# Expert gates of the second 128 tokens: scattered through DRAM in place of one-hot products

## Chip, cores and metric

One core of a Trainium2 chip runs the whole kernel. The metric is the device time of one execution in microseconds, the median of several runs.

## What is computed

A streaming encoder of two layers on 256 tokens of 1024 values. Each layer has an attention mixer and then a channel mixer, product-key expert retrieval (PEER), which the change is about. Cut to that:

```python
q = einsum('td,de->te', xt, w_q).reshape(t, 8, 2, 128)
sc = einsum('thpd,hpnd->thpn', q, sub_keys)            # 8 heads, 2 sides, 128 keys
v1, i1 = top_k(sc[:, :, 0], 16);  v2, i2 = top_k(sc[:, :, 1], 16)
cand = v1[..., :, None] + v2[..., None, :]
top_v, top_pos = top_k(cand.reshape(t, 8, 256), 16)
eidx = (i1 * 128 + i2) at top_pos                      # 16384 experts
gates = softmax(top_v, axis=-1)
a = gelu(einsum('tkd,td->tk', u_tab[eidx], xt)) * gates
out = einsum('tk,tkd->td', a, v_tab[eidx])
```

Each token has 8 heads x 16 = 128 experts of 16384. An expert is a pair of keys (i1, i2).

## The kernel before, in words

The kernel gathers nothing. It computes all 16384 experts for all tokens and multiplies by a gate matrix that is zero where an expert was not chosen. The experts are walked in 128 tiles, a tile j holding the 128 experts of one second key. Tiles go through two stages in each layer.

**Up stage.** For tile j, SyncE loads the tile of u (512 KB) into one of four buffers `raw`; ScalarE rounds it to the upper part `hi` (`split`, line 1119), VectorE takes the remainder `lo` (`lower`, line 1550), and TensorE multiplies both with the tokens (`x_both`, upper and lower part). Tiles 0 to 55 are "wide": one product of 512 columns and one of 256 for each of 8 slices, 16 in all, and VectorE adds the two halves (`sum_halves`, line 1618). Tiles from 56 are "up" tiles with 24 products of 256 columns. After Gelu on ScalarE, SyncE stores the tile's 128x256 result in DRAM (`spill`, to `s_store`). A tile's u is loaded when the subtraction for the tile four before is done, its split is two tiles ahead of TensorE.

**Down stage.** For each tile SyncE fetches the stored activations and a tile of v, VectorE multiplies by the gates (`weigh`, line 1562), and TensorE accumulates 12 products of 512 columns. In layer 0 the weights of layer 1 are loaded into the freed parts of the gate matrix at the same time, by GpSimd's queue.

**The gate matrix** `gates` takes all of the big buffer `big` (128 partitions x 128 tiles x 256 tokens, 16.8 MB): the first key runs over partitions, the second over tiles j. It can be written only when the retrieval's scratch, which lies in the same buffer, is no longer needed. It is made so:

- *Retrieval* on VectorE (`retrieve_head`, `top16`): the best 16 of each side and of the candidates, for 8 heads. It is cut into pieces that are issued between the subtractions of the tiles, by a generator (`retrieval`, `advance(500)` twice a step; a piece yields its nominal nanoseconds, and a step takes pieces until 500 are reached).
- *Selection* (`choose`, line 1506): the place of each chosen pair among the top 16 of either side is turned into keys by 32 selections `q_hots` of 128x256 values each (line 1533), and the gates by an Exp on ScalarE (line 1202, ahead of wide tile 52) and a division.
- *Sums* (`picks`, line 793): behind up tile 57, TensorE adds the 16 selections of each side in 64 bf16 products of 128 columns and so turns them, and the gates by two transposes, to have the 128 chosen experts on partitions and the tokens along the row. VectorE copies the three results into `pick`.
- *Groups* (`one_hot` line 1552, `group` line 837, `copy_gates` line 1156): for four tokens VectorE writes one-hot matrices of the first key and, times the gates, of the second; TensorE multiplies the two with one product of 128x128x128 for each token; ScalarE copies the four 128x128 results into `gates`. There are 64 groups, one in each up tile from tile 60 (`GROUP_AT`) to 123.

**Order around the change.** SyncE's queue issues loads of u, spills, loads of v and fetches in program order, with a wait ahead of each. GpSimd's queue issues the loads of the projection weights, `w_out`, the keys and `w_q`, and is idle while a layer's tiles run, but for layer 1's weights in layer 0's down stage. ScalarE and VectorE run a fixed order by tile; VectorE's first `weigh` follows the last subtraction of the up stage and a wait for all groups' copies (`g_copied`). Products are recorded under the helper's line 541.

Of the kernel before, what the change touches and what calls it, by code (L numbers as in the profile page):

```python
# [41 lines left out]
GROUPS = T // 4  # L42
GROUP_AT = 60
EXP_AT = 52
# [22 lines left out]
C_END = 3 * P  # L67
# [112 lines left out]
def build(nc, a, out):  # L180

    with ExitStack() as ctx:
# [23 lines left out]
        pick = wmod_ring[:, 2, 0:3 * T].rearrange("p (a t) -> p a t", a=3)  # L206
# [14 lines left out]
        iota = cst[:, C_IOTA:C_IOTA + P]  # L221

# [43 lines left out]
        s_store = nc.dram_tensor("s_store", (NKEY, P, T), F32, kind="Internal").ap()  # L266
        gates = big[:].rearrange("p (j t) -> p j t", j=NKEY)
# [26 lines left out]
        def q_area(at, size, **kw):  # L294
# [14 lines left out]
        q_idf = q_area(Q_IDF, 512, t=TT, h=PH, s=2, k=TOPK)  # L309
        q_ab = [q_area(at, 256).bitcast(U32) for at in (Q_A, Q_B, Q_TMP, Q_TMP + 256)]  # L310
        q_tmp = [q_area(Q_TMP + 256 * n, 256) for n in (2, 3, 4)]
        q_abf = [q_area(Q_AF, 256, t=TT, n=P), q_area(Q_BF, 256, t=TT, n=P)]
# [33 lines left out]
                 "q_ps", "q_copied", "key_ps", "key_copied", "sel_ready", "pick_copied",  # L346
                 "hot_ready", "hot_used", "g_copied", "hi_done", "lo_done", "w_used",
                 "s_gelu", "a_ready", "ah_done", "al_done",
                 "e_act", "e_dve", "eT_ps", "x_done")
        s = [{n: sem(f"{n}_{l}") for n in names} for l in range(LAYERS)]  # L350
        for n in ("s_half", "s_sum", "oh_done", "ol_done", "o_used", "yh_done", "yl_done", "xh_done", "xl_done", "gate_max", "gate_exp", "pick_ready", "pick_ps"):
            s[0][n] = s[1][n] = sem(n)
# [4 lines left out]
        mod_kept = sem("mod_kept")  # L357
        norm_names = ("sq_ready", "ss_ps", "rec_ready", "root_ready", "rms_ready", "rms_ps", "hat_ready", "h_ready")
# [18 lines left out]
        def _(sp):  # L377
# [16 lines left out]
            for l in range(LAYERS):  # L394
# [93 lines left out]
        def _(pool):  # L488
            for l in range(LAYERS):
# [34 lines left out]
                for h in range(PH):  # L524
# [10 lines left out]
                    pool.dma_start(big[:, at:at + 2 * D], a["w_q"][l, :, h * 2 * D:(h + 1) * 2 * D]).then_inc(wq_in[h % WQ_RING], 16)  # L535


        @block.tensor
        def _(pe):
# [212 lines left out]
            def queries(l):  # L752
                def sub_scores(h):
                    pe.wait_ge(s[l]["q_copied"], 2 * h + 2)
                    pe.wait_ge(keys_in, 16 * (l + 1))
                    if h >= 2:
                        pe.wait_ge(s[l]["key_copied"], h - 1)
# [34 lines left out]

            def picks(l):
                pe.wait_ge(ident_ready, 1)
                for n in range(4):
                    t, side = n // 2, n % 2
                    pe.wait_ge(s[l]["sel_ready"], TOPK * (side + 1))
                    c = side * T + t * P
                    for k in range(TOPK):
                        mm(bank[6][:, c:c + P], q_hot[n][:, k].rearrange("p h k -> p (h k)"), ident_bf, k == 0, k == TOPK - 1)  # L800
                pe.wait_ge(s[l]["pick_ready"], l + 1)
                for t in range(TT):
                    last = nc.tensor.transpose(bank[7][:, t * P:(t + 1) * P], q_g[:, t].rearrange("p h k -> p (h k)"), ident)
                last.then_inc(s[l]["pick_ps"], 1)

            def experts(l):
# [84 lines left out]
            def expert_out(l):  # L891
                for m in range(KT):
                    if m % 4 == 0:
                        pe.wait_ge(s[l]["e_act"], 1 + m // 4)
                        pe.wait_ge(s[l]["e_dve"], 1 + m // 4)
# [41 lines left out]
        def _(act):  # L937
# [30 lines left out]
            def norm(i, out_halves=()):  # L968
                if i == 0:
                    act.wait_ge(x_in, 16)  # L970
                for k in range(KT):
                    for q in out_halves[2 * max(k - 2, 0):2 * max(k - 1, 0)] if k >= 4 else out_halves[k:k + 1]:
                        split_out(i // 2, q)
                    if i:
                        act.wait_ge(s[(i - 1) // 2]["x_mixed" if i % 2 else "x_done"], k + 1)
# [99 lines left out]
            for l in range(LAYERS):  # L1075
# [91 lines left out]
                def copy_keys(h):  # L1167
                    act.wait_ge(s[l]["key_ps"], h + 1)
                    f(q_key[:, h].rearrange("p s t n -> p (s t n)"), bank[6 + h % 2][:, :], ACT.Copy).then_inc(s[l]["key_copied"], 1)

                for h in range(PH):
                    for side in range(2):
# [12 lines left out]
                        if h >= 2:  # L1185
                            act.wait_ge(s[l]["key_ps"], h - 1)
# [11 lines left out]
                with act.Fori(1, EXP_AT // 4) as i:  # L1198
                    for r in range(4):
                        wide_step(4 * i + r, r, i)  # L1200
                act.wait_ge(s[l]["gate_max"], l + 1)
                f(q_e[:], q_e[:], ACT.Exp).then_inc(s[l]["gate_exp"], 1)
                for n in range(EXP_AT, WIDE_TILES):
                    wide_step(n, n % 4, n // 4)
                sum_gelu(WIDE_TILES - 1, (WIDE_TILES - 1) % 4)
                up_steps(WIDE_TILES, GROUP_AT)
                act.wait_ge(s[l]["pick_copied"], 2)
                with act.Fori(0, GROUPS // 4) as i:
                    for r in range(4):
                        up_step(GROUP_AT + 4 * i + r, r, i + GROUP_AT // 4)  # L1210
                        copy_gates(4 * i + r, r)
                for r in range(4):
# [22 lines left out]
        def _(dve):  # L1235
# [256 lines left out]
            def retrieve_head(l, h):  # L1492
                dve.wait_ge(s[l]["key_copied"], h + 1)
# [12 lines left out]
            def choose(l):  # L1506

                v.tensor_tensor(q_e[:], q_top[:], q_top[:, :, :, 0:1].to_broadcast([P, TT, PH, TOPK]), ALU.subtract)\
                    .then_inc(s[l]["gate_max"], 1)

                pos = q_pos[:].rearrange("p t h k -> p (t h k)")
                far, d1, d2 = q_tmp
                v.tensor_single_scalar(q_ab[0], pos, 4, ALU.logical_shift_right)
                yield 600
                v.tensor_single_scalar(q_ab[1], pos, 15, ALU.bitwise_and)
                v.tensor_single_scalar(q_ab[2], pos, 2, ALU.logical_shift_right)
# [338 lines left out]
```

## Time and profile before

| what | before |
|---|---|
| time, median of 3 runs | 2010.26 us (2008.14 to 2011.47) |
| span of the profiled execution | 2004.7 us (5.6 under the median: what lies around the span) |
| TensorE busy | 1966.7 us, 98% |
| VectorE busy | 1554.3 us, 78% |
| ScalarE busy | 1104.4 us, 55% |
| GpSimd busy | 28.2 us, 1% |
| DMA moved | 446.88 MB, mean 223 GB/s |

The profile shows one execution. Busy time of an engine counts its instructions alone; matmuls are pipelined, so an engine that is always busy may still differ in how many products it ends in a time, and the period from one tile to the next says more. The DMA share is the mean busy share of the core's 16 DMA engines.

### The profile page before, as it was taken

To read this page: it belongs to the slowest core of one execution; us is meant where nothing else is said; L and a number is where in the kernel's file an instruction comes from. 1 tells how busy PE (TensorE), PEld (TensorE's weight loads), DVE (VectorE), ACT (ScalarE), POOL (GpSimd) and SP (SyncE) were. 2 spreads that over 40 slices of the span, in tenths; PEclk is the share of its full clock that TensorE was granted. 3 is DMA by queue.
4 is the path that set the end of the run, shared out by engine and by line. 5 is a ranking of instruction groups with operands and counts; after the bars stand their busy time and mean duration, and the time that the engine had idled before them with its cause. 6 is when DMAs were issued, how large, how long until landed. Compare 5 with 4: busy or idle time off the path is not lost.

```text
span 2004.7 us, 42800 instructions
## 1 busy us (share of the span) xinstructions
PE 1966.7 (98%) x12066; PEld 1740.0 (87%) x12066; DVE 1554.3 (78%) x3993; ACT 1104.4 (55%) x2231; POOL 28.2 (1%) x57
## 2 busy tenths in 40 slices
PE   7989999999999999999999999999999999999998
PEld 6748988899999888888888798889999998888887
DVE  5666799987777688888876568998777767777776
ACT  2035466655555555555555555666555555555554
POOL 1000000000000000000000000000000000000000
PEclk9999999999999999999999999999999999999999
DMA  9961299765556799999830435776555567777774
GB/s 368 375 234 50 93 311 299 264 189 174 177 170 174 255 337 339 331 342 331 292 119 1 190 127 178 236 237 207 178 174 172 175 207 240 241 240 243 239 243 164
DMA packets 171104, 446.88 MB, mean 223 GB/s; under 512 B 19088, under 2 KB 85904, under 8 KB 166944
## 3 DMA queue, kind: packets, MB, share of 16 engines
q1 hardware_dynamic: 163520, 392.65, 60.4%
q0 software_dynamic: 7520, 53.45, 6.9%
q8 instruction: 32, 0.52, 0.1%
q14 instruction: 32, 0.26, 0.0%
HBM read 409.32 MB, written 36.70 MB: 222 GB/s over the span
## 4 chain that ended last, share of the span: by engine, by line
PE 93%; DMA 2%; DVE 2%; ACT 2%; issue 1%; SPq 0%; DVEq 0%; ACTq 0%
PE bank L541 93%; DMA big<-in_w_mod 1%; ACT big L1050 1%; DMA big<-in_w_out 1%; DVE lo L1550 0%; DVE big L1533 0%; DMA raw<-in_v 0%; PE bank L677 0%; DVE raw L1264 0%; ACT hi L1119 0%; DVE big L1366 0%; DVE big L1272 0%; ACT hi L999 0%; DVE work L1618 0%; ACT raw L988 0%
## 5 line engine op out<-in xcount | busy, mean ns | idle before, releaser
L1550 DVE TENSOR_TENSOR lo<-raw,hi 128x512 fp32r<-128x512 f32 x1024 | 706.6, 690 | 274.5 <-ACT hi L1119 262.4
L541 PE MATMUL bank<-x_both,hi 128*128 128x256 f32 (+1 forms) x3984 | 886.8, 311 | 2.9 <-ACT x_both L966 1.5
L1119 ACT ACTIVATE hi<-raw 128x512 fp32r<-128x512 f32 x1024 | 643.9, 629 | 415.9 <-PE bank L541 388.3
L541 PE MATMUL bank<-x_both,lo 128*128 128x256 f32 x2440 | 685.8, 281 | 0.0
L541 PEld LDWEIGHTS bank<-x_both,hi 128*128 128x128 f32 x3984 | 647.4, 191 | 43.7 <-issue 2.4
L541 PEld LDWEIGHTS bank<-x_both,lo 128*128 128x128 f32 x2440 | 463.6, 190 | 0.0
L541 PE MATMUL bank<-hi,a_hi 128*128 128x512 f32 x1024 | 398.7, 389 | 1.5 <-DVE lo L1550 1.5
L541 PE MATMUL bank<-lo,a_hi 128*128 128x512 f32 x1024 | 398.6, 389 | 0.0
L541 PE MATMUL bank<-hi,a_lo 128*128 128x512 f32 x1024 | 398.5, 389 | 0.0
L541 PEld LDWEIGHTS bank<-hi,a_hi 128*128 128x128 f32 x1024 | 192.2, 188 | 41.6 <-issue 1.6
L541 PEld LDWEIGHTS bank<-hi,a_lo 128*128 128x128 f32 x1024 | 192.2, 188 | 39.9
L541 PEld LDWEIGHTS bank<-lo,a_hi 128*128 128x128 f32 x1024 | 192.2, 188 | 39.9
L1558 DVE TENSOR_SCALAR wmod_ring<-cst,wmod_ring 128x128 f32<-128x128 f32 x512 | 142.4, 343 | 0.0
L541 PE MATMUL bank<-wmod_ring 128*128 128x128 f32 x1024 | 135.2, 275 | 0.0
L541 PEld LDWEIGHTS bank<-wmod_ring 128*128 128x128 f32 x1024 | 125.7, 192 | 0.0
L1143 ACT ACTIVATE work<-bank 128x256 f32<-128x256 f32 x144 | 55.1, 382 | 112.7 <-PE bank L541 112.7
L1564 DVE TENSOR_TENSOR wmod_ring<-wmod_ring,big 128x256 f32<-128x256 f32 x256 | 107.5, 421 | 1.1
L541 PE MATMUL bank<-raw,big 128*128 128x256 f32 (+1 forms) x464 | 104.4, 383 | 3.7 <-ACT raw L988 3.7
L1569 DVE TENSOR_TENSOR a_lo<-wmod_ring,a_hi 128x256 fp32r<-128x256 f32 x256 | 107.2, 419 | 0.0
L541 PEld LDWEIGHTS bank<-raw,big 128*128 128x128 f32 (+1 forms) x464 | 85.7, 188 | 21.0 <-issue 8.3
L1165 ACT ACTIVATE a_hi<-wmod_ring 128x256 fp32r<-128x256 f32 x256 | 103.0, 403 | 0.0
L1555 DVE TENSOR_TENSOR wmod_ring<-cst,wmod_ring 128x512 f32<-128x512 f32 x128 | 87.6, 685 | 0.0
(161 smaller groups left out, 1330.0 us busy)
## 6 DMA issues: line engine op xcount, KB each, us to landing
raw<-in_u SPq DMA_DIRECT2D x256, 512.0 KB, 4.0
raw<-in_v SPq DMA_DIRECT2D x256, 512.0 KB, 4.6
s_store<-work SPq DMA_DIRECT2D x256, 128.0 KB, 3.7
wmod_ring<-s_store SPq DMA_DIRECT2D x256, 128.0 KB, 3.7
wmod_ring<-in_w_mod SPq DMA_DIRECT2D x54, 512.0 KB, 5.7
big<-in_w_mod SPq DMA_DIRECT2D x40, 512.0 KB, 6.4
big<-in_w_q POOLq DMA_DIRECT2D x16, 1024.0 KB, 7.4
big<-in_w_in POOLq DMA_DIRECT2D x5, 2048.0 KB, 21.4
```

Source lines behind the costliest of these rows:

```text
L541: return nc.tensor.matmul(o, w, x, start=start, stop=stop, skip_group_check=free)
L1050: last = f(c, c, ACT.Exp, bias=neg[:, 2 * i + t:2 * i + t + 1], accum_out=den[:, 2 * i + t:2 * i + t + 1])
L1119: f(hi[:, r % 2, c], raw[:, r, c], ACT.Copy).then_inc(s[l]["hi_done"], 1)
L1143: f(work[:, r, :], bank[4 + r % 2][:, 0:T], ACT.Gelu).then_inc(s[l]["s_gelu"], 1)
L1165: f(a_hi[:, r % 2, :], back[:, b, :], ACT.Copy).then_inc(s[l]["ah_done"], 1)
L1550: v.tensor_tensor(lo[:, r % 2, c], raw[:, r, c], hi[:, r % 2, c].bitcast(F32), ALU.subtract).then_inc(s[l]["lo_done"], 1)
L1555: v.tensor_tensor(hot[r % 2][:, 0], iota.unsqueeze(1).to_broadcast([P, 4, P]), pick[:, 0, bass.ds(4 * g, 4)].unsqueeze(2).to_broadcast([P, ...
L1558: ins = v.tensor_scalar(hot[r % 2][:, 1, n, :], iota, pick[:, 1, bass.ds(4 * g + n, 1)], pick[:, 2, bass.ds(4 * g + n, 1)], ALU.is_equal, ...
L1564: v.tensor_tensor(back[:, b, :], back[:, b, :], gates[:, bass.ds(j, 1), :].rearrange("p a t -> p (a t)"), ALU.mult)\
L1569: v.tensor_tensor(a_lo[:, r % 2, :], back[:, b, :], a_hi[:, r % 2, :].bitcast(F32), ALU.subtract).then_inc(s[l]["al_done"], 1)
```

## The change

The tokens 128 to 255 ("far") no longer pass through one-hot products. Their gates are added into a DRAM matrix `g_store` (8.4 MB, one for each layer), which SyncE has cleared before, by indirect DMAs on GpSimd's queue: one for each of the 128 chosen experts, which adds one gate of each of the 128 tokens at the place computed for it. Each head's 16 wait for the 16 of the head before. Then 16 loads bring the matrix into the far half of `gates`. The first 128 tokens keep the one-hot groups, now 32, from tile 68 to 99.

The selection goes in two waves of four heads, each right behind its heads' retrieval; the first wave's sums for far tokens are taken by TensorE ahead of wide tile 24, and VectorE computes places (`far_places`) at a fixed piece of head 4's retrieval. Each wave has its own Exp, ahead of tiles 16 and 60. VectorE waits for all far loads ahead of the first `weigh`. The far sums keep the tokens on partitions: the identity is the stationary operand and 64 columns of selections move.

Semaphores that had one counter for each layer now share one for both, so that their waits count on; the ring of descriptors of GpSimd's DMAs is set to 8192 bytes. In both layers the clear is one DMA of a 128x512 tile of zeros, repeated.

```diff
-GROUPS = T // 4
-GROUP_AT = 60
-EXP_AT = 52
+GROUPS = P // 4
+GROUP_AT = 68
+SCATTERED = T - P
+EXP_AT = (16, 60)
+FAR_PLACES_AT = (4, 9)
+SUM_AT = 24
+GATE_LOADS = 16
+ZERO_COLS = 512
...
+                def clear(n):
+                    sp.dma_start(g_store[n].rearrange("(a p f) o -> p a (f o)", p=P, f=ZERO_COLS),
+                                 zero[:].unsqueeze(1).to_broadcast([P, NKEY * SCATTERED // ZERO_COLS, ZERO_COLS])).then_inc(zeroed, 16)
+
                 if l == 0:
                     sp.wait_ge(s[0]["mod_tile"], NMOD)
                     sp.wait_ge(s[0]["map_max"], 16)
+                    sp.wait_ge(zero_ready, 1)
+                    sp.wait_ge(s[0]["prob_ready"], 2)
+                    clear(0)
                 sp.wait_ge(s[l]["x_mixed"], KT)
...
                 sp.dma_start(raw[:, 0:2].rearrange("p a n -> p (a n)"), x_store).then_inc(x_back, 16)
+                if l == 0:
+                    clear(1)
...
+            def scatter(l):
+
+                for h in range(PH):
+                    if h % 4 == 0:
+                        pool.wait_ge(s[l]["far_ready"], 4 * l + 2 * (h // 4 + 1))
+                    if h == 0:
+                        pool.wait_ge(zeroed, 16 * (l + 1))
+                    else:
+                        pool.wait_ge(s[l]["far_done"], 16 * TOPK * (PH * l + h))
+                    for k in range(TOPK):
+                        c = h * TOPK + k
+                        pool.indirect_dma_start(g_store[l], bass.IndirectOffsetOnAxis(ap=far_at[:, c:c + 1], axis=0), far_gate[:, c:c + 1], None,
+                                                compute_op=ALU.add).then_inc(s[l]["far_done"], 16)
+                pool.wait_ge(s[l]["far_done"], 16 * TOPK * PH * (l + 1))
+                pool.wait_ge(s[l]["pick_copied"], l + 1)
+                for n in range(GATE_LOADS):
+                    j = slice(n * NKEY // GATE_LOADS, (n + 1) * NKEY // GATE_LOADS)
+                    pool.dma_start(gates[:, j, P:T], g_store[l].rearrange("(j p t) o -> p j (t o)", j=NKEY, p=P)[:, j]).then_inc(s[l]["far_in"], 16)
...
+                scatter(l)
...
+            def far_sums(l, w):
+
+                pe.wait_ge(ident_ready, 1)
+                pe.wait_ge(s[l]["sel_ready"], 2 * TOPK * (2 * l + w + 1))
+                for side in range(2):
+                    o = bank[6][:, (2 * w + side) * 64:(2 * w + side + 1) * 64]
+                    for k in range(TOPK):
+                        last = mm(o, ident_bf, q_hot[2 + side][:, k, 4 * w:4 * w + 4].rearrange("p h k -> p (h k)"), k == 0, k == TOPK - 1)
+                last.then_inc(s[l]["far_ps"], 1)
...
+                far_sums(l, 1)
+                for side in range(2):
                     for k in range(TOPK):
-                        mm(bank[6][:, c:c + P], q_hot[n][:, k].rearrange("p h k -> p (h k)"), ident_bf, k == 0, k == TOPK - 1)
...
+                        mm(bank[7][:, side * P:(side + 1) * P], q_hot[side][:, k].rearrange("p h k -> p (h k)"), ident_bf, k == 0, k == TOPK - 1)
+                pe.wait_ge(s[l]["pick_ready"], 2 * l + 2)
+                nc.tensor.transpose(bank[7][:, 2 * P:3 * P], q_g[:, 0].rearrange("p h k -> p (h k)"), ident).then_inc(s[l]["pick_ps"], 1)
...
-                with pe.Fori(1, WIDE_TILES // 4) as i:
+                with pe.Fori(1, SUM_AT // 4) as i:
+                    for r in range(4):
+                        wide(4 * i + r, r)
+                far_sums(l, 0)
+                with pe.Fori(SUM_AT // 4, WIDE_TILES // 4) as i:
...
+                def gate_exps(w):
+                    act.wait_ge(s[l]["gate_max"], 2 * l + w + 1)
+                    c = q_e[:, :, 4 * w:4 * w + 4]
+                    f(c, c, ACT.Exp).then_inc(s[l]["gate_exp"], 1)
...
+                        v.scalar_tensor_tensor(out=q_hots[:, :, side, k, hs], in0=q_abf[side][:, w].rearrange("p t (h k) -> p t h k", k=TOPK), scalar=float(k),
+                                               in1=q_idf[:, w, :, :, side, k:k + 1].to_broadcast([P, TT, 4, TOPK]),
                                                op0=ALU.is_equal, op1=ALU.mult).then_inc(s[l]["sel_ready"], 1)
                         if k % 2:
-                            yield 800
...
+                            yield 500
...
+            def far_places(l, w):
+
+                dve.wait_ge(s[l]["far_ps"], 2 * l + w + 1)
+                o = bank[6][:, 2 * w * 64:2 * (w + 1) * 64].rearrange("p (s n) -> p s n", s=2)
+                link(v.tensor_scalar(far_tmp[:], o[:, 1], float(P * SCATTERED), row, ALU.mult, ALU.add))
+                v.scalar_tensor_tensor(out=far_at[:, 64 * w:64 * w + 64], in0=o[:, 0], scalar=float(SCATTERED), in1=far_tmp[:],
+                                       op0=ALU.mult, op1=ALU.add).then_inc(s[l]["far_ready"], 1)
...
+                        for n, took in enumerate(retrieve_head(l, h)):
+                            yield took
+                            if (h, n) == FAR_PLACES_AT:
+                                far_places(l, 0)
+                                yield 400
+                        if h % 4 == 3:
+                            yield from choose(l, h // 4)
...
                 dve.wait_ge(s[l]["g_copied"], GROUPS)
+                dve.wait_ge(s[l]["far_in"], 16 * GATE_LOADS * (l + 1))
```

## Rows read from the trace of the kernel before

**Rows 1.** The page: busy time of each engine; chain that ended last.

```profile
PE 1966.7 (98%) x12066; PEld 1740.0 (87%) x12066; DVE 1554.3 (78%) x3993; ACT 1104.4 (55%) x2231; POOL 28.2 (1%) x57
...
PE 93%; DMA 2%; DVE 2%; ACT 2%; issue 1%; SPq 0%; DVEq 0%; ACTq 0%
```

**Rows 2.** Windows by stage: engines' busy us (x instructions), PEclk, DMA share, GB/s.

```profile
150.00:191.00 41.00, 38.46 (x302) 35.92 (x302) 23.87 (x49) 20.25 (x40) 0.00 (x0) 1.00 0.06 24
...
250.00:400.00 150.00, 150.00 (x866) 130.78 (x865) 146.41 (x461) 100.51 (x213) 0.00 (x0) 1.00 0.87 290
...
425.00:665.00 240.00, 240.00 (x2041) 240.00 (x2040) 187.07 (x449) 135.76 (x255) 0.00 (x0) 1.00 0.59 175
...
700.00:1000.00 300.00, 300.00 (x1326) 248.41 (x1325) 256.88 (x579) 173.51 (x332) 11.61 (x22) 1.00 0.94 329
...
1030.00:1075.00 45.00, 43.72 (x305) 41.50 (x303) 25.10 (x49) 23.28 (x46) 0.00 (x0) 0.92 0.01 1
...
1230.00:1370.00 140.00, 140.00 (x810) 122.41 (x809) 133.20 (x449) 95.18 (x205) 0.00 (x0) 1.00 0.74 236
```

**Rows 3.** TensorE's timeline: first wide tile, two groups, two tiles without groups.

```profile
251.80 0.48 PE L541 MATMUL bank<-x_both,hi 128*128 128x512 f32 x1
...
428.98 1.06 PE L541 MATMUL bank<-wmod_ring 128*128 128x128 f32 x8
...
432.74 1.06 PE L541 MATMUL bank<-wmod_ring 128*128 128x128 f32 x8
...
670.04 0.40 PE L541 MATMUL bank<-x_both,hi 128*128 128x256 f32 x2
...
672.92 0.40 PE L541 MATMUL bank<-x_both,hi 128*128 128x256 f32 x2
```

**Rows 4.** Groups of instructions by form: busy us, mean ns.

```profile
L541 PE MATMUL bank<-wmod_ring 128*128 128x128 f32 x1024 | 135.2, 275 | 0.0
...
L1550 DVE TENSOR_TENSOR lo<-raw,hi 128x512 fp32r<-128x512 f32 x1024 | 706.6, 690 | 274.5 <-ACT hi L1119 262.4
...
L1533 DVE SCALAR_TENSOR_TENSOR big<-big 128x256 bf16<-128x256 f32 x64 | 24.4, 427 | 0.0
...
L1498 DVE TENSOR_TENSOR big<-big 128x128 f32<-128x128 f32 x16 | 4.6, 286 | 0.1
...
L1202 ACT ACT_TABLE_LOAD x2 | 2.6, 1283 | 0.0
...
L535 POOL DMA_DIRECT2D big<-in_w_q x16 | 8.4, 528 | 156.1 <-PE bank L541 156.1
```

**Rows 5.** TensorE's timeline: sums of the selections, layers 0 and 1.

```profile
417.43 2.85 PE L541 MATMUL bank<-par,big 128*128 128x128 bf16 x48 [1.82 <-DVE big L1533]
...
1379.63 3.75 PE L541 MATMUL bank<-par,big 128*128 128x128 bf16 x64
```

**Rows 6.** VectorE's timeline: second normalisation of layer 0.

```profile
140.22 2.15 DVE L1407 TENSOR_SCALAR big<-big,stat 128x128 f32<-128x128 f32 x8
```

**Rows 7.** Instructions on x_store: ns min/median/max, first and last start.

```profile
L415 SPq DMA_DIRECT2D x_store<-raw x2: 327/327/327, 191.0 to 1157.5; - x2
```

**Rows 8.** DMA issues: count, KB each, median us to landing.

```profile
raw<-in_u SPq DMA_DIRECT2D x256, 512.0 KB, 4.0
...
out_yT<-raw SPq DMA_DIRECT2D x4, 256.0 KB, 2.2
...
stat<-in_c SPq DMA_DIRECT2D x1, 4.0 KB, 1.6
```

**Rows 9.** DMA packets of 1275 to 1300 us, then of 275 to 300 us.

```profile
DMA packets 2579, 5.84 MB, mean 234 GB/s; under 512 B 289, under 2 KB 1441, under 8 KB 2579
...
q1 hardware_dynamic: 2579, 5.84, 73.3%
...
DMA packets 2997, 7.38 MB, mean 295 GB/s; under 512 B 333, under 2 KB 1482, under 8 KB 2997
...
q1 hardware_dynamic: 2997, 7.38, 90.6%
```

More of the change, by code:

```diff
@@ L66 @@
 C_ID, C_ONE, C_IOTA = 0, P, 2 * P
-C_END = 3 * P
+C_ROW = 3 * P
+C_END = C_ROW + 1
 def win_cols(l):
@@ L221, in build @@
         iota = cst[:, C_IOTA:C_IOTA + P]
+        row = cst[:, C_ROW:C_ROW + 1]
         def selector(h):
@@ L266, in build @@
         s_store = nc.dram_tensor("s_store", (NKEY, P, T), F32, kind="Internal").ap()
+        g_store = [nc.dram_tensor(f"g_store{l}", (NKEY * P * SCATTERED, 1), F32, kind="Internal").ap() for l in range(LAYERS)]
         gates = big[:].rearrange("p (j t) -> p j t", j=NKEY)
@@ L974, in norm @@
                     if i:
-                        act.wait_ge(s[(i - 1) // 2]["x_mixed" if i % 2 else "x_done"], k + 1)
+                        act.wait_ge(s[(i - 1) // 2]["x_mixed" if i % 2 else "x_done"], k + 1 if i % 2 else KT * ((i - 1) // 2) + k + 1)
                     if i or k >= 4:
@@ L1197, in _ @@
                     wide_step(n, n, 0, False, n >= 1)
-                with act.Fori(1, EXP_AT // 4) as i:
+                def gate_exps(w):
+                    act.wait_ge(s[l]["gate_max"], 2 * l + w + 1)
+                    c = q_e[:, :, 4 * w:4 * w + 4]
+                    f(c, c, ACT.Exp).then_inc(s[l]["gate_exp"], 1)
+                with act.Fori(1, EXP_AT[0] // 4) as i:
                     for r in range(4):
                         wide_step(4 * i + r, r, i)
[L1201 to L1204, printed above, removed]
+                gate_exps(0)
+                with act.Fori(EXP_AT[0] // 4, WIDE_TILES // 4) as i:
+                    for r in range(4):
+                        wide_step(4 * i + r, r, i)
                 sum_gelu(WIDE_TILES - 1, (WIDE_TILES - 1) % 4)
-                up_steps(WIDE_TILES, GROUP_AT)
-                act.wait_ge(s[l]["pick_copied"], 2)
+                up_steps(WIDE_TILES, EXP_AT[1])
+                gate_exps(1)
+                up_steps(EXP_AT[1], GROUP_AT)
+                act.wait_ge(s[l]["pick_copied"], l + 1)
                 with act.Fori(0, GROUPS // 4) as i:
@@ L1504, in retrieve_head, with choose, part @@
                                   for t in range(TT)])
[L1506 to L1523 removed]
+            def choose(l, w):
+                hs = slice(4 * w, 4 * w + 4)
+                c = slice(64 * w, 64 * w + 64)
+                def part(area):
+                    return area[:, 0:P].rearrange("p (t n) -> p t n", t=TT)
+                v.tensor_tensor(q_e[:, :, hs], q_top[:, :, hs], q_top[:, :, hs, 0:1].to_broadcast([P, TT, 4, TOPK]), ALU.subtract)\
+                    .then_inc(s[l]["gate_max"], 1)
+                pos = q_pos[:].rearrange("p t h k -> p t (h k)")[:, :, c]
+                far, d1, d2 = [part(x) for x in q_tmp]
+                ab = [part(x) for x in q_ab]
+                v.tensor_single_scalar(ab[0], pos, 4, ALU.logical_shift_right)
+                yield 400
+                v.tensor_single_scalar(ab[1], pos, 15, ALU.bitwise_and)
+                v.tensor_single_scalar(ab[2], pos, 2, ALU.logical_shift_right)
+                yield 400
+                v.tensor_single_scalar(ab[3], pos, 3, ALU.bitwise_and)
+                link(v.tensor_scalar(far, pos, float(WIDE * TOPK), None, ALU.is_ge))
+                yield 400
+                v.tensor_tensor(d1, ab[2], ab[0], ALU.subtract)
+                link(v.tensor_tensor(d2, ab[3], ab[1], ALU.subtract))
+                yield 500
@@ L1543, in choose @@
-                yield 1000
+                            yield 500
+                dve.wait_ge(s[l]["gate_exp"], 2 * l + w + 1)
+                total = gsum.rearrange("p (t h) -> p t h", t=TT)[:, :, hs]
+                share = grec.rearrange("p (t h) -> p t h", t=TT)[:, :, hs]
+                link(v.reduce_sum(total, q_e[:, :, hs], axis=AX_X))
+                link(v.reciprocal(share, total))
+                v.tensor_tensor(q_g[:, 0, hs], q_e[:, 0, hs], share[:, 0].unsqueeze(2).to_broadcast([P, 4, TOPK]), ALU.mult)\
+                    .then_inc(s[l]["pick_ready"], 1)
@@ new lines, in choose @@
+                v.tensor_tensor(far_gate[:, c].rearrange("p (h k) -> p h k", k=TOPK), q_e[:, 1, hs],
+                                share[:, 1].unsqueeze(2).to_broadcast([P, 4, TOPK]), ALU.mult).then_inc(s[l]["far_ready"], 1)
+                yield 700
+            def far_places(l, w):
[4 more added lines that the diff above has]
+                                       op0=ALU.mult, op1=ALU.add).then_inc(s[l]["far_ready"], 1)
```

76 lines of the change are left out of this document (31 added, 45 removed).

## The prediction

> **What bounds the kernel now.** Read first the page's busy line and chain: TensorE is busy 98% of 2004.7 us and holds 93% of the chain of waits that ended last [rows 1]. An instruction taken off TensorE is worth its full length, as long as nothing else becomes late. Next the windows by stage: in both expert stages TensorE is busy in all of every stretch, its granted clock 1.00, and the DMA engines' share runs from 0.59 to 0.94 [rows 2]. VectorE is nearly full in the first layer's wide tiles (146.4 of 150 us) but not in the group tiles (187 of 240). So the one-hot groups are paid for on TensorE, and the reserve that the change draws on is DMA time and GpSimd, which is all but idle (28 us).
>
> TensorE's timeline prices a group. Two groups of consecutive tiles start at 428.98 and 432.74, so a tile with a group takes 3.76 us; tiles without one start at 670.04 and 672.92, 2.88 us [rows 3]. A group costs 0.88 us.
>
> **The change part by part.** The sum is made against the profiled execution, whose span is 2004.7; the median of 2010.26 is 5.6 us (0.28%) over it, and I put the difference on top unchanged.
>
> *Groups.* 64 become 32 in each layer: 64 x 0.88 = 56.3 us less. The x1024 row holds all of them: 512 products, two records each [rows 4]. VectorE's one-hots and ScalarE's copies for them fall away too and were hidden.
>
> *Sums of the selections.* Before, 64 bf16 products take 3.75 us, 0.059 each [rows 5]. After, there are 32 of that form and 64 with half the columns, one transpose fewer. Half-width products cost between half and all of a full one: 0 to 1.9 us more a layer. I take 1.0, so +2. In layer 0 they were interrupted by 1.82 us of waiting for VectorE's selections [rows 5]; that wait may stay or go, I take 0.9 off.
>
> *Selection on VectorE.* From the code: 151 pieces of retrieval and selection become 175, spread two to a step over 66 steps instead of 58; as before, only the last one or two are left when the steps end. A 256-element selection takes 427 ns, a 128-element operation 286 [rows 4], so 64 x 286 replaces 32 x 427, 4.6 us more a layer, but each piece is cheaper and the eight added steps have room: two subtractions of 690 ns in a 2.88 us tile. If that cover failed, TensorE would wait up to those 4.6 us at the sums. I cost it at nothing.
>
> *New waits.* TensorE's first sums, before tile 24, need selections that VectorE issues in step 19 (layer 0) and 22 (layer 1); tile 24 itself needs step 22. VectorE's read of them stands at step 26 or 28, with the subtractions for later tiles queued behind, and two tiles of distance. ScalarE's first Exp at tile 16 needs step 7 or 13. Each Exp brings two table loads of 1.28 us [rows 4], so one more pair a layer on an engine with 50 of 150 us free [rows 2]: 0 to 2.6 us a layer, I take 0.3, +0.6.
>
> *Clearing.* 8.4 MB from SP in layer 0 goes out when the second normalisation ends, at 142.4; SP's next issue, the store of x, is at 191.0 [rows 6, 7]. The engines' share between 150 and 191 is 0.06 [rows 2]. At the 329 GB/s that the down stage moves [rows 2] it takes 26 us, w_q's and the keys' loads beside it (5.2 MB) 16 more: over by 185. The second clear goes behind the read of x at the layer's end, where the share is 0.01 to 1075. Nothing, in both; without that cover the store and the load of u behind it would be up to 26 us late.
>
> *Scatters.* On GpSimd, 64 a wave, behind w_q's issues and ahead of the next layer's weights, which wait for the down stage anyway. No row shows an indirect DMA. From below: a plain issue is 0.53 us [rows 4]. From above: issue plus landing of a small one, 0.53 + 1.6 for 4 KB, 0.53 + 2.2 for the output's [rows 4, 8]: 2.13 to 2.73. The sixteen of a head do not wait for each other, so the issue is the nearest row, but each has 128 addresses; I take 1.3, plus 2.2 at the end of each head: 64 x 1.3 + 9 = 92 us a wave. Wave one of layer 0 starts near tile 27, 251.8 + 27 x 2.77 (16 records a tile, 866 in 150 us) = 327, and ends at 419. Wave two starts after the second sums, 251.8 + 56 x 2.77 + 10 x 2.88 + 5 = 441, and ends at 534. The up stage, whose last tile ended at 672.92 + 2 x 2.88 = 679, will end near 651.
>
> *Loading back.* 16 loads, 8.4 MB in 16384 pieces of 512 B, between 534 and 651, beside u and the spills. Two windows price a packet: they differ by 377 of 4 KB and by 17.3% of 16 x 25 us, so 0.18 us each; the first then leaves 0.074 us for each of its 1152 packets of 1 KB [rows 9]. A 512 B packet costs between half and all of that: 38 to 76 us with all engines. Free are 0.41 of the 33 us with groups left and 0.29 of the 82 without (0.74 at 2.77 us a tile is 0.71 at 2.88): 37 us. By bytes there is more: 329 GB/s ran without hurting TensorE, which leaves 154 GB/s and 102 GB/s, 13.5 MB against 8.4. I take it to fit, near the lower price, at 2 us a layer for u's loads held up: +4.
>
> **Sum:** -56.3 + 2 - 0.9 + 0.6 + 4 = -50.6. Span 1954, time 2010.3 - 50.6 = **1960**. Without the loads' 4 it is 1956.
>
> **A rule weighed.** The rows say that a small transfer is nearly all overhead: 4 KB lands after 1.6 us, 512 KB after 4.0 [rows 8]. The Trainium skill ("DMA: Bandwidth & Descriptors", its rules for kernel authors) says the same, to coalesce because under 64 KB one pays mostly overhead, and its anatomy of the gpsimd path gives about 2.0 us fixed, most of it the landing's receipt. It speaks against 256 transfers of 512 bytes. Paid by each in turn it would make 128 x 2.0 = 256 us a layer, an estimate by that page, and give rival B; paid once a head, as I assume, it agrees with the sum.
>
> **Rivals.** A, the loads come late but the groups still win. At a packet price midway, 0.055, they need 56 us of engines against 37 free: VectorE's new wait ahead of the first gate product holds the down stage for 19 us a layer, 1956 + 38 = 1994. For it: spare engine time is no more than the lowest need. Against: the bytes.
>
> B, slower: GpSimd is the bound. If a scatter takes c, both waves of a layer run end to end from 327, 327 + 128c + 18. At 2.13 that is 618, the loads find 33 us with 10 us of engine time, 28 are left for after the last tile, and 1956 + 56 = 2012: no gain, which is the point from which it decides. At 2.4 the waves end at 652 and all 38 us lie open, 1956 + 2 x 39 = 2034, the time I give B; at 2.73 they end at 694, 2 x 81 more, 2118. For it: 2.13 is only issue plus one landing, and VectorE holds two 690 ns subtractions in each tile; a scatter that had to let one pass would cost 1.3 + 0.69 = 1.99, just short of the point. The Trainium skill ("SBUF — State Buffer", who interferes with whom) has such a rule: a VectorE instruction with two SBUF inputs blocks a GpSimd instruction that reads SBUF; no run here shows it. Against B: the code queues sixteen at a time.
>
> C, the change does not do what it says: the saved TensorE time goes to another engine. A tile without a group asks 2 x 0.69 us of VectorE against 2.88 of TensorE, ScalarE is busy 136 of 240 us even with groups [rows 2], and such tiles do run at 2.88, so only a coincidence of small losses gives 2010.
>
> **How the numbers follow.** Sum right, 0.47, with its own range 1949 (no cost for sums, Exp and loads, the wait gone, a little less pressure on VectorE) to 1972. A 0.20, B 0.27, C 0.06. The range reaches to A and to B as priced, up to 2035, which leaves out B's dearer prices, under 0.2. Within 0.2% (4 us, about what a measurement of this kernel can tell from none) is C: 0.06; faster 0.67; slower 0.27.
>
> **What would show it.** In the after trace: 512 records of the group product in place of 1024; up tiles without groups at 2.88; POOL's indirect issues with a mean under 1.6 us; the last gate load landing before the last up tile ends, with no gap of TensorE behind it. A gap there, put down to a DMA into big, is A or B: A if the second wave's last scatter was issued by about 540, B if near 620 or later. Wrong altogether: group tiles that stay at 3.76 where only u runs, u's loads landing much later than 4.0 us in the stretch of the loads, or a wait of TensorE before tile 24.

## The result, and the profile after

The changed kernel takes **2012.6 us** in the median of 8 runs, the kernel before 2007.7 in 8 runs beside it: ratio 1.0031, 95% interval 1.0019 to 1.0042, a little slower. The forecast was 1960, faster. What came is rival B, GpSimd as the bound, at the time of the point from which it decides (2012) and not at the time it was given (2034). The profiled executions have spans of 2009.3 and 2004.7 us.

The page of the changed kernel, busy time and chain of waits [rows 1]:

```profile
PE 1916.6 (95%) x11616; PEld 1687.5 (84%) x11616; DVE 1462.3 (73%) x3779; ACT 1121.2 (56%) x2217; POOL 482.7 (24%) x346
...
PE 58%; POOL 21%; issue 10%; DMA 6%; DVE 3%; ACT 2%; SPq 0%; ACTq 0%; DVEq 0%; POOLq 0%
```

TensorE has 50.1 us less to do (1966.7 - 1916.6). But the chain, 93% TensorE before, now runs through GpSimd for a fifth of the span. The windows of the up and down stage of layer 0 show where the gain is paid back (columns as in [rows 2]):

```profile
425.00:665.00 240.00, 227.41 (x1936) 226.48 (x1934) 147.17 (x326) 125.43 (x236) 156.23 (x102) 0.98 0.84 214
...
625.00:650.00 25.00, 24.12 (x199) 23.77 (x199) 11.73 (x17) 12.25 (x25) 9.45 (x11) 1.00 1.03 356
650.00:675.00 25.00, 6.91 (x58) 6.70 (x56) 1.39 (x2) 2.77 (x6) 1.84 (x3) 0.69 0.99 327
675.00:700.00 25.00, 22.32 (x87) 18.26 (x88) 18.76 (x41) 12.49 (x25) 1.10 (x2) 0.84 0.68 222
```

TensorE stands nearly still from 656 to 678 us while the DMA engines are busy in all of the stretch. Its timeline there, and the row of layer 1:

```profile
656.63 0.28 PE L585 MATMUL bank<-x_both,lo 128*128 128x256 f32 x1
677.68 0.76 PE L585 MATMUL bank<-hi,a_hi 128*128 128x512 f32 x1 [20.78 <-ACT a_hi L1218]
678.25 0.63 PE L585 MATMUL bank<-lo,a_hi 128*128 128x512 f32 x1
678.67 0.63 PE L585 MATMUL bank<-hi,a_lo 128*128 128x512 f32 x1
...
1645.09 0.77 PE L585 MATMUL bank<-hi,a_hi 128*128 128x512 f32 x1 [27.78 <-ACT a_hi L1218]
```

The first products of the down stage come 20.8 and 27.8 us after TensorE was ready, and the first dozen (nine in layer 1) 0.43 us apart instead of 0.23: the granted clock is 0.69 in the window with the gap and 0.84 in the next, a mix of its two levels of 1.2 and 2.4 GHz, after TensorE had been idle. VectorE's waits name the cause, GpSimd's timeline shows it being made:

```profile
DVE wmod_ring L1644 <- DMA big<-g_store: 49.7, 2, 27.4
```

```profile
331.98 1.65 POOL L523 DMA_INDIRECT g_store<-far_gate,far_at  x1 [109.33 <-DVE far_at L1622]
...
484.08 1.54 POOL L523 DMA_INDIRECT g_store<-far_gate,far_at  x1 [2.43 <-DMA g_store<-far_gate,far_at]
...
615.90 1.54 POOL L523 DMA_INDIRECT g_store<-far_gate,far_at  x1 [0.30 <-issue]
617.75 1.76 POOL L523 DMA_INDIRECT g_store<-far_gate,far_at  x1 [0.31 <-issue]
622.12 6.29 POOL L529 DMA_DIRECT2D big<-g_store  x7 [2.61 <-DMA g_store<-far_gate,far_at]
643.95 6.13 POOL L529 DMA_DIRECT2D big<-g_store  x7 [15.55 <-issue]
667.93 1.76 POOL L529 DMA_DIRECT2D big<-g_store  x2 [17.84 <-issue]
```

The 128 scatters of layer 0 run without a pause between the waves (the second begins at 484) from 332 to 618, the 16 loads behind them are issued from 622 to 670 in three batches, and the last lands near 675, 18 us after the last up tile ended. The group of all scatters, by form, gives their price:

```profile
L523 POOL DMA_INDIRECT g_store<-far_gate,far_at x256 | 425.5, 1662 | 372.0 <-DVE far_at L1622 223.5 <-issue 105.8 <-DMA g_store<-far_gate,far_at 42.6
```

That is 1.66 us each and 0.30 us of "issue" behind each (idle time for which the profile shows no cause). To this come 3.0 us of waiting at a head's end for the landing of its last scatter (42.6 in 14), and beyond the 0.30s some 34 us of stops inside heads (105.8 - 240 x 0.30, both layers).

### The profile page after: what moved, and what is told of

Its sections match the earlier page's. It is cut to its first block, busy times and chain, and to the rows that moved or that the text cites. A ratio compares the mean times of both kernels' runs of the same rounds, so it can differ in the third digit from the quotient of the medians.

```text
span 2009.3 us, 41296 instructions
## 1 busy us (share of the span) xinstructions
PE 1916.6 (95%) x11616; PEld 1687.5 (84%) x11616; DVE 1462.3 (73%) x3779; ACT 1121.2 (56%) x2217; POOL 482.7 (24%) x346
## 2 busy tenths in 40 slices
DMA packets 220811, 480.72 MB, mean 239 GB/s; under 512 B 56496, under 2 KB 123312, under 8 KB 216640
## 4 chain that ended last, share of the span: by engine, by line
PE 58%; POOL 21%; issue 10%; DMA 6%; DVE 3%; ACT 2%; SPq 0%; ACTq 0%; DVEq 0%; POOLq 0%
PE bank L585 57%; POOL g_store L523 20%; DMA g_store<-far_gate,far_at 3%; POOL big L529 1%; DVE lo L1630 1%; ACT big L1103 1%; DMA big<-in_w_out 1%; DMA big<-g_store 1%; DMA raw<-in_x 0%; DMA raw<-in_u 0%; PE bank L721 0%; DMA raw<-x_store 0%; ACT hi L1172 0%; DVE wmod_ring L1671 0%; DVE raw L1325 0%
## 5 line engine op out<-in xcount | busy, mean ns | idle before, releaser
L523 POOL DMA_INDIRECT g_store<-far_gate,far_at x256 | 425.5, 1662 | 372.0 <-DVE far_at L1622 223.5
L585 PE MATMUL bank<-hi,a_hi 128*128 128x512 f32 x1024 | 400.5, 391 | 48.6 <-ACT a_hi L1218 48.6
L1474 DVE TENSOR_TENSOR lo<-big,hi 128x512 fp32r<-128x512 f32 x76 | 52.1, 689 | 32.7 <-ACT hi L1010 32.4
L1638 DVE TENSOR_SCALAR wmod_ring<-cst,wmod_ring 128x128 f32<-128x128 f32 x256 | 73.2, 375 | 0.0
L585 PE MATMUL bank<-big 128*128 128x128 f32 (+5 forms) x368 | 59.4, 326 | 9.3 <-ACT big L1121 8.3
## 6 DMA issues: line engine op xcount, KB each, us to landing
g_store<-zero SPq DMA_DIRECT2D x2, 8192.0 KB, 30.7
```

What stands on the lines that cost most here:

```text
L523: pool.indirect_dma_start(g_store[l], bass.IndirectOffsetOnAxis(ap=far_at[:, c:c + 1], axis=0), far_gate[:, c:c + 1], None, compute_op=ALU ...
L585: return nc.tensor.matmul(o, w, x, start=start, stop=stop, skip_group_check=free)
L1474: v.tensor_tensor(lo[:, q % 4 // 2, c], narrow_half(l, q), hi[:, q % 4 // 2, c].bitcast(F32), ALU.subtract).then_inc(s[l]["ol_done"], 1)
L1638: ins = v.tensor_scalar(hot[r % 2][:, 1, n, :], iota, pick[:, 1, bass.ds(4 * g + n, 1)], pick[:, 2, bass.ds(4 * g + n, 1)], ALU.is_equal, ...
```

## Experiments

Times stand beside runs of the kernel before on the same chip, in three groups (medians 2005.6, 2005.4, 2005.2; the last experiment's single run beside 2005.7). Experiments 1, 4 and 6 have two runs, the others but the last four to eight. The changed kernel was not run beside them: the ratio to hold against theirs is its 1.0031.

**1. Half the scatters.** For each head only k = 0 to 7:

```
-                    for k in range(TOPK):
+                    for k in range(KEPT):        # KEPT = 8, the counts waited for accordingly
```

> Leaves out the scatters of the picks 8 to 15 of every head (half of the gates of the second 128 tokens); all else as after the change. Theory G (the chain on GpSimd: 128 scatters at 1.66 + 0.30 us, eight landings of about 3.6 us, then the loads, sets when the down stage starts): 64 scatters and eight landings are 154 us a layer, the second wave starts when its addresses are ready at about 450 and ends near 527, the loads end before 600, far ahead of the last up tile at 656; the gaps of TensorE ahead of the down stage (20.8 and 27.8 us) and the lower clock behind them go: 2011 - 49 - 5 = 1957. Rival E (the loads and the scatters cost TensorE its time because the DMA engines are full, wherever they stand): the loads hold up u's loads instead, the up stage gets 10 to 20 us longer a layer, 1977 to 1997.

Measured 1959.2 us, ratio 0.9767 (0.9725 to 0.9809). GpSimd's scatters of layer 0 (count, ns min/median/max, first and last start) and the windows where the gap was:

```profile
L524 POOL DMA_INDIRECT g_store<-far_gate,far_at x64: 1535/1544/2082, 335.5 to 521.8; - x64
```

```profile
625.00:650.00 25.00, 25.00 (x211) 25.00 (x210) 11.95 (x18) 13.44 (x27) 0.00 (x0) 1.00 0.80 239
650.00:675.00 25.00, 25.00 (x148) 22.25 (x147) 18.43 (x38) 14.63 (x29) 0.56 (x1) 1.00 0.95 317
```

As theory G has it: the loads are issued from 527 to 570, no gap is left, and the granted clock stays at 1.00. Loads that come this early cost TensorE nothing.

**2. Waiting for a quarter of the loads.**

```
-                dve.wait_ge(s[l]["far_in"], 16 * GATE_LOADS * (l + 1))
+                dve.wait_ge(s[l]["far_first"], 16 * FIRST_LOADS * (l + 1))     # 4 of 16
...
+                        if first:                                # ahead of down step 24 or 28
+                            dve.wait_ge(s[l]["far_in"], 16 * (GATE_LOADS - FIRST_LOADS) * (l + 1))
```

> Same outputs as the changed kernel: VectorE waits for 4 of the 16 loads ahead of the first gate product, for the other 12 ahead of the 26th (layer 0) or 30th (layer 1). Theory G: the first four loads are issued within 4 us of the last scatter's landing at 622 and land by about 640, before the last up tile at 656; the gap of both layers goes, the other twelve land by about 690, ahead of the tile that needs them (656 + 26 x 2.7 = 726): 1955 to 1962. Rival E (full DMA engines): the loads then compete with v's, s's and the modulation's, the first down tiles wait for DMA instead, and only part of the gap returns: 1975 to 2000.

1987.2 us, 0.9904 (0.9879 to 0.9928): half of what theory G expected, in rival E's range. TensorE's timeline in layer 0:

```profile
650.40 0.47 PE L586 MATMUL bank<-x_both,hi 128*128 128x256 f32 x2 [1.79 <-ACT work L1197]
...
655.29 0.48 PE L586 MATMUL bank<-x_both,hi 128*128 128x256 f32 x2 [1.79 <-ACT work L1197]
...
668.02 0.77 PE L586 MATMUL bank<-hi,a_hi 128*128 128x512 f32 x1 [5.26 <-DVE a_lo L1650]
```

Up tiles now follow each other in 4.89 us where 2.88 is normal, since u's tiles and the spills of s land late (ScalarE's waits there: 6.9 us on u, 7.2 on the spills, 9.7 on v), and 5.3 and 9.0 us of gap remain. So the start of the loads isn't all. That their rate is too much beside the rest is a suspicion here, which experiments 8 and 9 test.

**3. Twice the descriptor memory.**

```
-    nc = bacc.Bacc("TRN2", ..., dynamic_dma_scratch_size=8192)
+    nc = bacc.Bacc("TRN2", ..., dynamic_dma_scratch_size=16384)      # ZERO_COLS = 256 for room
```

> Twice the memory for GpSimd's DMA descriptors (16384 bytes a partition instead of 8192), and the clear written in pieces of 1 KB instead of 2 KB to make room; all else as after the change. Rival R (the ring of descriptors holds 7 of the loads and GpSimd idles 33 us a layer until it empties): 15 or 16 loads are issued in one go in about 14 us, the last lands about 33 us earlier, near 645, both gaps go, about 1960. Theory G with full engines under the loads (DMA share 1.0, 340 GB/s, of which u and the spills take about half): the issues come together, but the last load still lands within 5 us of 675, and the time stays within 2003 to 2013.

1993.6 us, 0.9946 (0.9928 to 0.9964): neither. GpSimd's timeline:

```profile
616.35 13.27 POOL L529 DMA_DIRECT2D big<-g_store  x15 [3.10 <-DMA g_store<-far_gate,far_at]
658.47 0.88 POOL L529 DMA_DIRECT2D big<-g_store  x1 [28.84 <-issue]
```

Fifteen loads instead of seven go out in one batch, so the memory does set the batch; the sixteenth waits 28.8 us. In 625 to 650 us the engines are full (1.03) and TensorE has 20.3 us of 25 where it had 24.1: part of what the gap gave back is taken from the up stage. Gaps of 4.1 and 6.3 us remain ahead of the down stages.

**4. Even and odd heads in two matrices**, so that a head waits for the head but one before it.

```
-                        pool.wait_ge(s[l]["far_done"], 16 * TOPK * (PH * l + h))
+                    if h >= 2:
+                        pool.wait_ge(s[l][f"far_done{h % 2}"], 16 * TOPK * (PH // 2 * l + h // 2))
```

> Even heads are added into one matrix of DRAM, odd heads into a second one that is cleared with it and not loaded back (leaves out half of the gates of the second 128 tokens); a head waits for the landing of the head but one before it. Rival B (the landings between heads are what is lost): the 6 of 8 landings between heads that held GpSimd, about 3.6 us each, go, scatters end about 22 to 25 us earlier, near 598, the loads end near 650, the gap of layer 0 goes and layer 1 keeps about 3: 1962 to 1968. If instead the scatters' own pace on GpSimd or the DMA engines' pace of 4-byte additions is the limit: the period rises above 1.96 us and the last scatter stays later than 612, 1990 to 2010. The second clear takes the engines 31 us longer near 150 and 1030 us and may hold up the store of x there by up to 12 us in layer 0; that is read from its own row and taken off.

1965.4 us, 0.9798 (0.9766 to 0.983).

```profile
L525 POOL DMA_INDIRECT g_store<-far_gate,far_at x64: 1534/1543/2562, 331.4 to 549.2; - x64
L525 POOL DMA_INDIRECT g_odd<-far_gate,far_at x64: 1542/1542/4143, 365.1 to 579.1; - x64
```

The last scatter starts at 579 instead of 618, 39 us earlier, more than the landings' 22: the stops inside heads are gone too. The store of x was issued at 190.7 and landed in 8.8 us at most, so the second clear cost at most 5 us there. One matrix, with its landings and stops together, thus costs a seventh of the scatters' 286 us.

The time lies in rival B's range, in part by luck: the scatters end 19 us sooner than it said, but the loads, issued from 585 on, take 4.3 us of TensorE's time out of the up stage of layer 0, with the engines full:

```profile
600.00:625.00 25.00, 21.81 (x178) 21.26 (x177) 9.69 (x14) 10.69 (x23) 6.13 (x7) 1.00 1.02 354
625.00:650.00 25.00, 23.90 (x197) 23.75 (x198) 12.47 (x18) 13.48 (x28) 1.76 (x2) 1.00 0.99 345
```

**5 to 7. Larger pieces.** The matrix laid out by partition and the gates on chip in blocks of eight rows, so that a load is 128 pieces of 4 KB instead of 1024 of 512 B:

```
-        gates = big[:].rearrange("p (j t) -> p j t", j=NKEY)
+        gates = big[:].rearrange("p (b s i t) -> p b s i t", b=GATE_LOADS, s=2, t=P)
...
-                    pool.dma_start(gates[:, j, P:T], g_store[l].rearrange("(j p t) o -> p j (t o)", j=NKEY, p=P)[:, j])
+                    pool.dma_start(gates[:, n, 1], g_store[l].rearrange("(p j t) o -> p j (t o)", p=P, j=NKEY)[:, j])
```

With the wait of the second experiment, then alone, then with that wait and the larger memory of the third:

> Same outputs as the changed kernel. The matrix in DRAM and the gates on chip are laid out so that a load is 128 pieces of 4 KB instead of 1024 of 512 B, and VectorE waits for 4 of 16 loads first, as in the second experiment (1987). Theory P (what the loads cost beside u is their 16384 pieces): the engines' need falls from some 29 to some 20 us (by 159 ns for a 4 KB packet), the ring no longer stops GpSimd, up tiles during the loads stay at 2.88 and the first gate product finds its loads landed: 1957 to 1968. Theory Y (it is bytes: up stage and loads together ask for more than the 350 GB/s that the engines moved there): the stretching of the last up tiles to 4.9 us per pair of half tiles and the late v loads stay, 1980 to 1990.

> Same outputs; only the layout of the experiment before (loads of 128 pieces of 4 KB), with one wait for all 16 loads as in the changed kernel. Theory P: 16 loads issued within 10 us of the last landing at 622, all landed by about 650, gaps of TensorE ahead of the down stage gone in layer 0 and under 8 us in layer 1: 1958 to 1975. Theory Y: 8.4 MB at the 130 GB/s that were left beside u need 64 us or take u's share; up tiles stretch and the gap stays in part: 1985 to 1997, as with the larger ring (1994).

> Same outputs; pieces of 4 KB, the wait for the first 4 loads, and the larger ring (with the clear in 1 KB pieces) together. The larger ring let the last scatter be issued 6 us earlier in layer 0 and 12 in layer 1 in the third experiment; if the start of the loads still decides, this one is 3 to 12 us faster than the one without it; if the loads are hidden already there, the same within 3 us.

1987.1 us, 0.9904 (0.9881 to 0.9927); 1990.5, 0.9921 (0.9901 to 0.9941); 1980.5, 0.9872 (0.9856 to 0.9889). The fifth and the sixth lie in theory Y's ranges. Beside the second experiment, pieces of 4 KB bring no time, though they move more while the engines are full. The same window of the second and of the fifth:

```profile
625.00:650.00 25.00, 22.60 (x187) 22.22 (x185) 9.70 (x14) 10.45 (x21) 9.69 (x11) 1.00 1.01 336
625.00:650.00 25.00, 24.21 (x202) 24.03 (x201) 10.52 (x16) 11.66 (x23) 7.30 (x15) 1.00 1.02 398
```

One part of theory P did come true: all 16 loads go out in one batch. Alone (the sixth) the new layout is worth 22 us against the changed kernel (0.9921 against 1.0031), the larger memory alone 17. In the seventh the scatters end 6 us (layer 0) and 11 us (layer 1) sooner than in the fifth, and it is 7 us faster, though the two intervals still touch: when the loads start still decides. TensorE's timeline and a window of one tile in the seventh:

```profile
648.00 0.48 PE L586 MATMUL bank<-x_both,hi 128*128 128x256 f32 x2 [0.99 <-ACT work L1197]
...
652.12 0.47 PE L586 MATMUL bank<-x_both,hi 128*128 128x256 f32 x2 [1.01 <-ACT work L1197]
...
648.00:652.12 4.12, 3.10 (x24) 2.93 (x25) 1.39 (x2) 1.55 (x4) 0.00 (x0) 1.00 1.03 414
```

One up tile takes 4.12 us while u, spills and loads move 414 GB/s: every engine is full.

**8 and 9. The loads spread out.** In the seventh kernel, and in the second (512 B pieces, small memory), one load per two tiles:

```
+                    pool.wait_ge(s[l]["w_used"], 2 * (PACE_AT + 2 * n))      # PACE_AT = 114
                     pool.dma_start(gates[:, ...
```

> Same outputs. The kernel of the seventh experiment (pieces of 4 KB, wait for the first 4 loads, larger ring; 1980), with the loads held back to one per two tiles: load n is issued when TensorE has finished tile 114 + 2n of the up and down stages. Theory Y (bytes at once: the loads as a burst move 416 GB/s with u and the spills and stretch the last up tiles from 2.88 to 4.1 us and make the first v and s late): at 512 KB per 5.8 us, 91 GB/s on top of 226, under the 350 to 416 seen, the up tiles stay at 2.88, the gap ahead of the down stage goes, and the time is that of the kernel without a late load, 1955 to 1965 (half of the scatters left out gave 1959). Rival S (the rest is not the burst but the scatters and sums themselves): within 4 us of 1980.

> Same outputs. The kernel of the second experiment (pieces of 512 B, small ring, wait for the first 4 loads; 1987) with the same pacing of the loads. Theory Y: the pieces' size matters little once the loads are spread out: the scatters end 6 to 12 us later and the first four loads come in a burst, so it loses up to 8 us a layer there: 1960 to 1975. If the many small pieces cost by themselves: 1978 to 1987.

**1962.9 us, 0.9784 (0.9771 to 0.9797)**, and 1967.0, 0.9806 (0.9791 to 0.9821). Both compute all that the changed kernel computes and are faster than it and than the kernel before. In the eighth, ahead of the down stage and behind it:

```profile
625.00:650.00 25.00, 25.00 (x211) 25.00 (x210) 12.09 (x18) 13.35 (x26) 2.11 (x4) 1.00 0.96 325
650.00:675.00 25.00, 24.50 (x131) 20.94 (x131) 18.83 (x41) 14.12 (x29) 2.63 (x5) 1.00 1.02 388
...
700.00:725.00 25.00, 23.48 (x102) 18.53 (x101) 19.49 (x46) 12.49 (x25) 3.65 (x7) 1.00 1.03 400
```

The up tiles keep their 2.88 us and the clock its 1.00, though the last scatter still starts at 613. The eighth differs from the seventh by this wait alone, the ninth from the second likewise, so it is the spreading that gave the 18 and 20 us. 1.5 us are lost at 700 to 725, where the next layer's weights, queued behind the loads on GpSimd, come at once (four pieces of 512 KB in 2.1 us of issuing at 701).

**10. Writes instead of additions.**

```
-                        pool.indirect_dma_start(g_store[l], ..., far_gate[:, c:c + 1], None, compute_op=ALU.add)
+                        pool.indirect_dma_start(g_store[l], ..., far_gate[:, c:c + 1], None)
```

> The 256 indirect DMAs write instead of adding (leaves out the additions: where two heads pick one expert for a token, the later gate replaces the earlier); everything else as after the change, the loads and their waits included. Theory G, in its finer form (GpSimd's 1.54 us and the 0.30 us behind it are the making of 128 descriptors, not the addition): the period inside a head stays 1.84 to 1.96 us, the last scatter is issued within 10 us of 618, the time stays 2000 to 2013. Rival A (the additions, which read before they write, hold the engines, and through them the landings and the ring): the landings at a head's end fall from 3.3 to under 2.5 us, the stops inside a head go, the engines' share at 575 to 600 us falls from 0.89 to about 0.80, scatters end 15 to 25 us earlier and the time is 1975 to 1995.

1957.1 us in one run, which has no interval (the two runs of experiment 1 are 10 us apart): theory G fell in its finer form, and rival A was too small.

```profile
L523 POOL DMA_INDIRECT g_store<-far_gate,far_at x256 | 290.1, 1133 | 362.2 <-DVE far_at L1621 244.7 <-issue 89.3 <-DMA g_store<-far_gate,far_at 28.2
```

```profile
409.09 1.21 POOL L523 DMA_INDIRECT g_store<-far_gate,far_at  x1 [1.78 <-DMA g_store<-far_gate,far_at]
...
450.55 0.96 POOL L523 DMA_INDIRECT g_store<-far_gate,far_at  x1 [13.35 <-DVE far_at L1621]
...
554.57 6.29 POOL L528 DMA_DIRECT2D big<-g_store  x7 [2.36 <-DMA g_store<-far_gate,far_at]
```

A write takes GpSimd 1.13 us, not 1.66. The first wave is done by 437, 13 us before the second one's addresses, and the loads start at 555: the forecast's course, 18 and 21 us later than its dates of 419 and 534, and still early enough to be hidden. Rival A's signs came in part: the engines' share at 525 to 550 us falls from 0.75 to 0.59, but a landing still takes 2.8 us (28.2 in 10), and some 17 us of stops inside heads remain (89.3 - 242 x 0.30).

## Why the prediction was wrong

*Groups.* Right: 512 records remain. With the late loads out of the way the time is 42 to 49 us under the kernel before beside it (experiments 8, 1 and 10), against the forecast's 50.6. That their 1957 to 1963 meet its 1960 is in part luck: it was reckoned from 2010.3, they stand beside some 2005.5.

*Sums.* Half-width products cost half (32 of them from 320.32 to the next tile at 321.26, 0.029 each against 0.059 [rows 5]); with them the sums of layer 0 take 0.9 + 4.3 us, of layer 1 about what they took, so +1.5 where +2 was forecast. But that is not the width, as the forecast had it: the 1.5 lies in layer 0 behind a wait of TensorE, where the granted clock is 0.66 (444 to 449 us). The wait for VectorE ahead of the second sums was to shrink to 0.9 us; it is 3.1 in layer 0 and 1.8 in layer 1 (line 1601, the selections). Missed by 4 us: 4.9 - 1.8 more, not 0.9 less.

*Selection.* Put at nothing, with a wait of TensorE at the sums named as what its failure would cost. The 3.1 and 1.8 us are that wait, so in part the cover failed.

*Exp and clearing.* Small, as forecast; no run prices the Exp by itself. The clear lands in 30.7 us (26 forecast); TensorE has 38.01 us of 41 in that window against 38.46 [rows 2].

*Scatters: the step that failed.* It took 1.3 us for each, from the plain issue up, and 2.2 a head: 92 us a wave, so that the waves would be done at 419 and 534. Measured are 1.66 + 0.30, 3.0 at a head's end and the stops: 2.27 us each over a layer ((622 - 332) / 128), 152 us for the first wave, 138 for the second, and the end at 622. The forecast's 1.3 is close to a scatter that *writes* (1.13 + 0.30). No row of before shows an addition in DRAM, and the step put the addition at nothing; experiment 10 prices it at 0.53 us of GpSimd for each scatter, and with landings and stops at 2.27 against 1.63 ((554.57 - 450.55) / 64). Which part of an addition holds GpSimd is not shown.

In rival B's own terms, which set the landings of the heads apart as 18 us, the measured scatter costs (622 - 332 - 18) / 128 = 2.13: its point, with the times it named there, 618 for the end and 2012 for the kernel. The mechanism was B's, the meeting of the numbers is in part luck. B's 2.13 was one issue and one landing for each scatter, which is not how the time is made up, and its 56 us were all waiting for loads, where the gaps are 48.6 and the rest is the clock behind them and the sums.

*The start of the second wave.* At 450 its addresses were ready (441 forecast), but the first wave was not over, so this date decided nothing.

*Loading back.* Forecast: hidden for +4. It is hidden if it begins by about 555: in experiment 1 TensorE is busy in all of every window while the loads run, in experiment 10 it loses 0.1 us in layer 0 and 1.5 in layer 1. From 585 on (experiment 4) they take 4.3 us of the up stage. From 622 on it takes 53 us, with the engines full; for 16 and 18 of them GpSimd idles between batches. Neither larger pieces nor the larger memory alone cured that (experiments 3 and 6); spreading the loads, with a first wait for four of them, did. To count bytes, as the prediction did, was right in kind, but it counted them over 117 us; in the 35 that were left, its 102 GB/s make 3.6 MB of the 8.4.

*The rule weighed.* Its 2.0 us for each small transfer, from the Trainium skill ("DMA: Bandwidth & Descriptors", its anatomy of the gpsimd path), lies nearer to the measured 2.27 than the 1.3 + 2.2 a head that I took (1.44 each): 256 us a layer by that estimate, 290 measured. But the traces show another make-up than a landing paid by each: scatters of a head follow each other every 1.85 us (615.90 to 617.75) without waiting for one.

*The port rule* of the Trainium skill ("SBUF — State Buffer", who interferes with whom). Here the trace agrees in sign only: scatters take 1.75 us on average at 330 to 400 (30 in 52.6 us), where VectorE is nearly full with subtractions of two inputs, and 1.55 at 455 to 555 (45 in 69.7). That is 0.2, not 0.69; the DMA engines' share differs as well (0.98 and 0.75), and no run separates the causes. With writes (experiment 10) the sign is gone: 1.11 in the first wave (70.8 in 64), where VectorE is busy 98 of 105 us, and 1.16 in the second (74.3 in 64).

**The balance.** TensorE's busy time fell by 50.1 us: 56.3 of groups, less 1.5 at the sums and some 4.6 of products at the lower clock behind the gaps (2.6 and 2.0, by their spacing). Its idle time rose from 38.0 (2004.7 - 1966.7) to 92.7 us: 48.6 of gaps ahead of the down stages, 3.1 at the sums, the other 3.0 in small waits. 54.7 - 50.1 = 4.6 us, the longer span.

What stays open is why GpSimd stops for 2 to 6 us inside some heads. The larger memory lessened it (10 us instead of 17 in layer 0), two matrices ended it.

## What to carry to other kernels

Work moved to an idle engine is free only while its whole chain, with each landing it must wait for and the loads behind it, ends before the stage that hid it; so put the chain's start, its price per piece and its end on one time line. Where no row shows the price of a piece, ask what the piece does that the nearest row does not: here it was the addition, left at nothing. Where loads must come late, let the reader wait for the first few only, and pace the rest: 8.4 MB at once behind one wait cost 25 us a layer here, the same bytes one load per two tiles little (1.5 and 0.5 us of layer 0 in experiment 8).

## What the runs showed that was not expected

- An indirect DMA that adds holds GpSimd 1.66 us for 128 addresses, one that writes 1.13; packets under 512 B per scatter are 146 against 34 ((56496 - 19088) / 256 and (27824 - 19088) / 256, from the pages' counts).
- Additions take DMA engines, not bandwidth: at 575 to 600 us the changed kernel shows a share of 0.89 for 211 GB/s, the first experiment, with its scatters over by then, 0.80 for 226 at 600 to 625. With writes in place of additions the share at 525 to 550 is 0.59 for 181 GB/s, with additions 0.75 for 176.
- A load of 1024 pieces takes GpSimd 0.88 us and goes out in batches of 7 (15 with twice the memory); one of 128 pieces takes 0.53, and all 16 go out at once.
- After a gap of 21 or 28 us the granted clock of the window fell to 0.69 and 0.52; after one of 2.7 us in the seventh experiment it was 0.93.
